# The recurrence of an RWKV-7 layer: receptance products in quarters behind the first pair's features, least distances in the written order, reciprocals in pieces of 64 columns

## The reference, cut to what matters

```python
kk = kk / jnp.maximum(jnp.sqrt(jnp.sum(kk * kk, axis=-1, keepdims=True)), 1e-12)
k_dir = k[None] * (1.0 + (a - 1.0) * k_a)
def step(s, inp):
    r_t, w_t, kk_t, a_t, k_t, v_t = inp
    s_kk = jnp.einsum('bhvk,bhk->bhv', s, kk_t)
    s = (s * w_t[:, :, None, :] - s_kk[..., None] * (kk_t * a_t)[:, :, None, :]
         + v_t[..., None] * k_t[:, :, None, :])
    return s, jnp.einsum('bhvk,bhk->bhv', s, r_t)
# output of a head: (y - mean) / sqrt(var + eps), scaled, plus (r . k_dir) v, times a gate
```

## Time and profile before

| | us |
|---|---|
| median of three runs | 3086.72 (3081.71 to 3093.74) |
| profiled execution | 3085.09 |
| its span | 3083.5 |

### The profile page before, as it was taken

How to read it: one execution, slowest core, us unless ns; L and a number is a source line. 1 busy time by engine, 2 the same in 40 slices (tenths; PEclk the granted TensorE clock), 3 DMA queues, 4 the chain that set the end, 5 groups by cost and what they waited for, 6 DMA issues and landing times. The chain is left out here.

```text
span 3083.5 us, 62817 instructions
## 1 busy us (share of the span) xinstructions
PE 2859.8 (93%) x26751; PEld 2331.1 (76%) x26751; DVE 1897.7 (62%) x3016; ACT 1428.7 (46%) x2197; POOL 526.2 (17%) x482
## 2 busy tenths in 40 slices
PE   7899899998899889999889999999989977999999
PEld 2795677777778658887549999999956744678877
DVE  4941565555665257765778888888864256466652
ACT  1212555655554242221347777777734345343231
POOL 1001545545542010000010000000010045100000
PEclk9999999999999999999999999999989988999999
DMA  5553000000000277655249999999922210222222
GB/s 206 193 191 127 23 21 21 21 21 21 3 3 4 82 255 277 267 198 199 87 153 424 367 369 363 369 367 372 366 99 105 87 36 19 89 77 96 96 96 82
DMA packets 73843, 482.11 MB, mean 156 GB/s; under 512 B 11107, under 2 KB 13027, under 8 KB 32144
## 3 DMA queue, kind: packets, MB, share of 16 engines
q1 hardware_dynamic: 59360, 418.48, 36.0%
q0 software_dynamic: 11952, 51.91, 4.6%
q10 hardware_dynamic: 2304, 8.39, 0.7%
HBM read 457.20 MB, written 34.13 MB: 159 GB/s over the span
## 5 line engine op out<-in xcount | busy, mean ns | idle before, releaser
L2360 DVE TENSOR_TENSOR sb_moe_w_lo<-w_ring,sb_moe_w_hi 128x1408 fp32r<-128x1408 f32 (+1 forms) x132 | 255.3, 1934 | 69.9 <-ACT sb_moe_w_hi L2305 68.3
L2208 PE MATMUL ps<-sb_moe_w_hi,sb_x_feat_lo 128*128 128x352 f32 x832 | 273.4, 329 | 5.2 <-DVE sb_moe_w_lo L2360 5.1
L2210 PE MATMUL ps<-sb_moe_w_hi,sb_x_feat_hi 128*128 128x352 f32 x832 | 267.5, 321 | 0.0
L2209 PE MATMUL ps<-sb_moe_w_lo,sb_x_feat_hi 128*128 128x352 f32 x832 | 266.8, 321 | 0.0
L2305 ACT ACTIVATE sb_moe_w_hi<-w_ring 128x2816 fp32r<-128x2816 f32 x80 | 204.3, 2554 | 2.5 <-DMA w_ring<-w_moe_up 1.8
L2208 PE MATMUL ps<-sb_moe_w_hi,sb_hid_feat_lo 128*128 128x256 f32 x572 | 163.2, 285 | 3.9 <-DVE sb_hid_feat_lo L2491 3.9
L2208 PEld LDWEIGHTS ps<-sb_moe_w_hi,sb_x_feat_lo 128*128 128x128 f32 x832 | 156.1, 188 | 11.5 <-issue 10.4
L2210 PE MATMUL ps<-sb_moe_w_hi,sb_hid_feat_hi 128*128 128x256 f32 x572 | 161.8, 283 | 0.0
L2209 PE MATMUL ps<-sb_moe_w_lo,sb_hid_feat_hi 128*128 128x256 f32 x572 | 161.8, 283 | 0.0
L2209 PEld LDWEIGHTS ps<-sb_moe_w_lo,sb_x_feat_hi 128*128 128x128 f32 x832 | 157.0, 189 | 0.0
L2210 PEld LDWEIGHTS ps<-sb_moe_w_hi,sb_x_feat_hi 128*128 128x128 f32 x832 | 156.0, 187 | 0.0
(11 more groups left out here) (540 smaller groups left out, 7751.2 us busy)
## 6 DMA issues: line engine op xcount, KB each, us to landing
w_ring<-w_moe_up SPq DMA_DIRECT2D x67, 1408.0 KB, 8.4
sb_hm<-w_ada SPq DMA_DIRECT2D x48, 1024.0 KB, 7.1
w_ring<-w_ffn SPq DMA_DIRECT2D x22, 1024.0 KB, 4.9
w_ring<-w_up SPq DMA_DIRECT2D x22, 1024.0 KB, 4.8
sb_b_again<-w_moe_up SPq DMA_DIRECT2D x13, 1408.0 KB, 8.6
sb_hm<-w_moe_up SPq DMA_DIRECT2D x13, 1408.0 KB, 8.2
sb_t_again<-w_moe_up SPq DMA_DIRECT2D x13, 1408.0 KB, 7.7
w_ring<-w_moe_down SPq DMA_DIRECT2D x13, 1408.0 KB, 7.3
```

The source lines that it names most:

```text
L2208: pe.matmul(out, x_lo, w_hi, start=first, stop=False)
L2209: pe.matmul(out, x_hi, w_lo, start=False, stop=False)
L2210: return pe.matmul(out, x_hi, w_hi, start=False, stop=end)
L2360: return V.tensor_tensor(WL[:, s, w], raw[raw_at(c, i)[0]][:, w], WH[:, s, w].bitcast(F32), ALU.subtract)
```

## The change

- The receptance tiles are cut in quarters (two of eight products each), divmod(j, 4) giving tile and part. Two quarters stand ahead of pair 0's Pw0, one ahead of each of Pw1, Pa0, Pa1 and Pnorm, nine ahead of Pg, six ahead of Gkds. The other eleven, with pair 0's Pv and Av0 to Av3 behind the third of them, stand ahead of every second rec entry of the first quad; until they are used up, no feature of pair 1 is placed.
- The tiles come in the order FIRST = (0, 1, 4, 5, 6, 7, 2, 3), and the last three share PSUM bank 5. Loads of r wait for the tile's place in that order. The first score waits for five tiles, the score of the second quad for all eight. The ten keep-warm products are gone.
- behind gives least distances, in rec entries: Pmean 8 behind Gy, Pvar 4 behind Asq, Dbonus 3 behind Pcoef, Pw0 5 behind Dbonus.
- Reciprocals are cut in pieces of 64 columns: twelve for a feature, eight for an output, where six and four were.
- Av is four entries, Av0 to Av3 (waits on v become waits on v3, waits on the output's rec3 waits on rec7), and Pv with them moves from ahead of GB to the end of main.

```diff
@@ -941,8 +941,10 @@
...
 SC_CUTS = ((0, 256), (256, 512), (512, 768))
-REC_CUTS = tuple((a, a + P) for a in range(0, TOK, P))
-OUT_CUTS = tuple((a, a + P) for a in range(0, SEQ, P))
+REC_CUTS = tuple((a, a + CH) for a in range(0, TOK, CH))
+OUT_CUTS = tuple((a, a + CH) for a in range(0, SEQ, CH))
+
+FIRST = (0, 1, 4, 5, 6, 7, 2, 3)
 
@@ -954,10 +956,10 @@
...
         "Asq", "Dscan1.0", "Pnorm", "Dscan1.1", "Aroot", "Dscan1.2", "Gex1", "Drec0", "Gin1", "Drec1", "Drec2",
-        "Drec3", "Drec4", "Drec5", "Dkkn", "APx0", "APi0", "APx1", "APi1", "AP0", "Gkka", "AP1", "APe", "GA", "Pg",
-        "Ag", "Pv", "Av", "GB", "Akd0", "Akd1", "Ark", "Gkdk", "GK", "GR", "Gkds", "Gcoefin"]
+        "Drec3", "Drec4", "Drec5", "Drec6", "Drec7", "Drec8", "Drec9", "Drec10", "Drec11", "Dkkn", "APx0", "APi0", "APx1", "APi1", "AP0", "Gkka", "AP1", "APe", "GA", "Pg",
+        "Ag", "GB", "Akd0", "Akd1", "Ark", "Gkdk", "GK", "GR", "Gkds", "Gcoefin", "Pv", "Av0", "Av1", "Av2", "Av3"]
 late = ["Pcoef", "Dbonus"]
-outs = ["Gy", "Pmean", "Dyc", "Asq", "Pvar", "Aroot", "Drec0", "Drec1", "Drec2", "Drec3", "Gyn", "Aaff", "Gbonus",
+outs = ["Gy", "Pmean", "Dyc", "Asq", "Pvar", "Aroot", "Drec0", "Drec1", "Drec2", "Drec3", "Drec4", "Drec5", "Drec6", "Drec7", "Gyn", "Aaff", "Gbonus",
         "Gated"]
@@ -995,13 +997,17 @@
...
 
+behind = {"Pmean": ("Gy", 8), "Pvar": ("Asq", 4), "Dbonus": ("Pcoef", 3), "Pw0": ("Dbonus", 5)}
 plan, turn = [], 0
 for x in main:
-    if x in ("Pw0", "Pw1", "Pa0", "Pa1", "Pnorm", "Pg"):
-        for n in range(turn, turn + 1 + (x in ("Pnorm", "Pg"))):
-            plan.append(("receptance", 0, n))
-        turn = n + 1
-    plan.append(("feature", 0, x))
+    n = {"Pw0": 2, "Pw1": 1, "Pa0": 1, "Pa1": 1, "Pnorm": 1, "Pg": 9, "Gkds": 6}.get(x, 0)
+    plan += [("receptance", 0, divmod(j, 4)) for j in range(turn, turn + n)]
+    turn += n
+    if x[1:2] != "v":
+        plan.append(("feature", 0, x))
+values = [("feature", 0, x) for x in main if x[1:2] == "v"]
+spare = [("receptance", 0, divmod(j, 4)) for j in range(turn, 4 * 6)] + values + [
+    ("receptance", 0, divmod(j, 4)) for j in range(4 * 6, 4 * N)]
 for p in range(N):
@@ -1019,17 +1025,24 @@
...
         quiet |= {i for i in range(start, ends[q]) if rec[i][1].rstrip("0123456789.") in FRONT[:3]} | set(range(ends[q] - 6, ends[q]))
-    first, turn, stop = 4, ends[0], len(rec) - 16
-    done = [0, 0]
+    first, turn, stop = 8, ends[0], len(rec) - 16
+    done, at_step = [0, 0], {}
     for i, x in enumerate(rec):
+        if p == 0 and i % 2 == 0 and spare:
+            plan.append(spare.pop(0))
+        if spare:
+            plan.append(("rec", *x))
+            continue
         for at, (side, lo, hi) in enumerate(((early, first, turn - 8), (after, turn, stop))):
...
                 continue
-            while done[at] < len(side) and (done[at] < due and (side[done[at]][2][0] != "G" or i not in quiet)
+            while done[at] < len(side) and i - at_step.get(behind.get(side[done[at]][2], ("", 0))[0], -P) >= behind.get(
+                    side[done[at]][2], ("", 0))[1] and (done[at] < due and (side[done[at]][2][0] != "G" or i not in quiet)
                                             or done[at] and side[done[at]][2] in ("Aw0", "Aw1", "Aa0", "Aa1")
...
                 plan.append(side[done[at]])
+                at_step[side[done[at]][2]] = i
                 done[at] += 1
@@ -1113,7 +1126,8 @@
...
             def r_load(p):
-                sp.wait_ge(s_rst[p % 4], 16 * (p // 4 + 1))
+                j = FIRST.index(p)
+                sp.wait_ge(s_rst[j % 4], 16 * (j // 4 + 1))
                 sp.dma_start(r2[:, p % 2, :], A["r_rows"][p]).then_inc(s_r2[p % 2], 16)
@@ -1210,7 +1224,7 @@
...
                 if x == "yn":
-                    pool.wait_ge(o_dve.sem, o_dve.at("rec3", p))
+                    pool.wait_ge(o_dve.sem, o_dve.at("rec7", p))
                     return G.tensor_tensor(YS[:, 0, :], YS[:, 0, :], YS[:, 1, :], ALU.mult)
@@ -1295,7 +1309,7 @@
...
                     pe.wait_ge(o_act.sem, o_act.at("root", p - 2))
-                act("v")
+                act("v3")
                 pe.wait_ge(f_pool.sem, f_pool.at("coefin", p))
@@ -1314,15 +1328,18 @@
...
                 if kind == "receptance":
-                    w = ring.all[:, 2 * KT * P * (x // 2):2 * KT * P * (x // 2 + 1)]
-                    if x % 2 == 0:
-                        pe.wait_ge(s_wr[x // 2], 16)
-                    if x >= 6:
-                        pe.wait_ge(s_re, x - 5)
-                    for k in range(KT):
-                        last = pe.matmul(ps[:, x % 6, :], w[:, (2 * k + x % 2) * P:(2 * k + x % 2 + 1) * P], xr[:, k, :],
+                    j, part = x
+                    m = FIRST[j]
+                    w = ring.all[:, 2 * KT * P * (m // 2):2 * KT * P * (m // 2 + 1)]
+                    if part == 0:
+                        pe.wait_ge(s_wr[m // 2], 16)
+                        if j > 5:
+                            pe.wait_ge(s_re, j)
+                    for k in range(2 * part, 2 * part + 2):
+                        last = pe.matmul(ps[:, min(j, 5), :], w[:, (2 * k + m % 2) * P:(2 * k + m % 2 + 1) * P], xr[:, k, :],
                                          start=(k == 0), stop=(k == KT - 1))
-                    last.then_inc(s_r, 1)
+                    if part == 3:
+                        last.then_inc(s_r, 1)
                     continue
@@ -1348,11 +1365,10 @@
...
                     if n == 0:
-                        pe.wait_ge(s_re, KT)
-                        if p == 0:
-                            self.keep_warm(pe, 3, 10)
+                        pe.wait_ge(s_re, 5 if p == 0 else KT)
                         pe.wait_ge(f_pool.sem, f_pool.at("K", p))
                     if n == CCH:
+                        pe.wait_ge(s_re, KT)
                         pe.wait_ge(f_pool.sem, f_pool.at("R", p))
@@ -1406,7 +1422,7 @@
...
                     else:
-                        pe.wait_ge(f_act.sem, f_act.at("v", p))
+                        pe.wait_ge(f_act.sem, f_act.at("v3", p))
                     for d in range(2):
@@ -1494,17 +1510,15 @@
...
                     return S.activation(PE2[:, u, 1, :], cs[:, 1, :].rearrange("p (c t) -> p c t", t=CH)[:, :, 0], ACT.Copy)
-                if x == "v":
+                if x[0] == "v":
+                    parity, side = divmod(int(x[1]), 2)
                     pe("v")
...
                         act.wait_ge(pe_c.sem, pe_c.at(f"Y{NCH - 1}", p - 2))
-                    for parity, tokens in enumerate(heads):
-                        for side, hh in enumerate(heads):
-                            last = S.activation(
-                                VT[hh, u, :, :].rearrange("p (g c q) n -> p g c q n", g=2, c=3, q=2)[:, :, :, parity, :],
-                                ps[tokens, 6:8, 0:3 * P].rearrange("p g (c h n) -> p g c h n", c=3, h=2)[:, :, :, side, :],
-                                ACT.Copy)
-                    return last
+                    return S.activation(
+                        VT[heads[side], u, :, :].rearrange("p (g c q) n -> p g c q n", g=2, c=3, q=2)[:, :, :, parity, :],
+                        ps[heads[parity], 6:8, 0:3 * P].rearrange("p g (c h n) -> p g c h n", c=3, h=2)[:, :, :, side, :],
+                        ACT.Copy)
                 d = int(x[-1])
@@ -1526,12 +1540,15 @@
...
                 if kind == "receptance":
-                    act.wait_ge(s_r, x + 1)
-                    if x >= 4:
-                        act.wait_ge(s_rst[x % 4], 16)
-                    S.activation(RB[:, x % 4, :], ps[:, x % 6, :], ACT.Copy).then_inc(s_re, 1)
-                    act.wait_ge(s_re, x + 1)
-                    act.dma_start(A["r_rows"][x], RB[:, x % 4, :]).then_inc(s_rst[x % 4], 16)
+                    j, part = x
+                    if part < 3:
+                        continue
+                    act.wait_ge(s_r, j + 1)
+                    if j >= 4:
+                        act.wait_ge(s_rst[j % 4], 16)
+                    S.activation(RB[:, j % 4, :], ps[:, min(j, 5), :], ACT.Copy).then_inc(s_re, 1)
+                    act.wait_ge(s_re, j + 1)
+                    act.dma_start(A["r_rows"][FIRST[j]], RB[:, j % 4, :]).then_inc(s_rst[j % 4], 16)
                     continue
@@ -1588,11 +1605,11 @@
...
                 if x.startswith("rec"):
-                    lo, hi = REC_CUTS[int(x[3])]
+                    lo, hi = REC_CUTS[int(x[3:])]
                     dve.wait_ge(f_act.sem, f_act.at("root", p))
...
                 if x == "kkn":
-                    dve.wait_ge(f_dve.sem, f_dve.at("rec5", p))
+                    dve.wait_ge(f_dve.sem, f_dve.at("rec11", p))
                     return V.scalar_tensor_tensor(out=kk[:, :], in0=kk[:, :], scalar=1e12, in1=kq[:, :], op0=ALU.min, op1=ALU.mult)
```

(4 more changed lines are left out.)

## The result

The changed kernel takes 3092.16 us, median of 19 runs (3086.97 to 3096.79), against 3086.72 for the kernel before (median of 19, 3081.71 to 3094.25). The ratio is 1.0017, 95% interval 1.0010 to 1.0023: 5.4 us slower by the medians, where I had forecast 22.5 us gained. It lies within half a per cent of the kernel before, but above the upper end of my range (3084). The profiled execution's span is 3090.9, 7.4 above before's.

A forecast was written before the change was run, and what follows sets the result against it. TensorE was taken to bound the recurrence stage. Front 5.7, six pairs 15 and pairs 0 and 7 2, less 0.2 at the last output, gave 22.5 us gained: 3062.6 us (3064 against the median), range 3046 to 3084.

The forecast's parts named there:

- First score: Serial front ahead of the pairs: first score starts at 299.3 us, 24.3 earlier, with TensorE deciding.
- Second quad: End of pair 0's first quad: second quad starts at 346.3 instead of 352, gain 5.7 us, bounds 0 and 11.
- Pmean 1.1, Pcoef and Dbonus 1.0: Steady pairs: larger distances and later Pcoef cut TensorE's waits behind Gy, Gcoefin and Dbonus, by 1.1 and 1.0 us a pair.
- Reciprocals 0.5: Steady pairs: halved reciprocals block VectorE half as long, so W waits shrink; 0.5 us a pair, bounds -1 and 1.2.
- V copy 0.9: Steady pairs: V copy in four pieces of 0.49 us shortens X's waits behind ScalarE; 0.9 us a pair.
- The wait of an X behind ScalarE mostly goes: Steady pairs: splitting the V copy mostly removes TensorE's X waits behind ScalarE, 1.1 us a pair.
- Pcoef later: Steady pairs: Pcoef moves later, easing its wait behind Gcoefin; part of the 1.0 us a pair taken with Pw0 behind Dbonus.
- Exponentials 1.0, bounds 0 and 2.5: Third quad's scores: exponentials moved there delay Us of chunk 4 and TensorE's Y4; loss 1.0 us a pair.
- Pairs 0 and 7, 2 us: Pair 0 behind its first quad and pair 7 have part of the waits, together gaining 2 us.
- Period: Time from one steady pair to the next: falls below 87.0 us, to 84.5.
- my 3.5: Steady pairs: the gains 1.1, 1.0, 0.9 and 0.5 us a pair, before the exponentials' loss of 1.0.
- The rival of ScalarE's pile: Third quad's scores: 6.3 us of exponentials on ScalarE make K late and each pair's score wait; 3109 us, chance 0.08.

The follow-up runs named there:

- front_and_v: Changed kernel with whole reciprocals, no distances or empty entries, early part starting at 4 again; new front and V copy at list's end kept: pair 86.95 us, ratio 0.9972.
- whole_spread: The mid_root kernel with whole reciprocals of 128 columns, each followed by an empty entry: pair 85.10 us, ratio 0.9952.
- us_first: The mid_root kernel with one exponential moved behind the copy Us of chunk 4: pair 83.90 us, total 3064.13 us, ratio 0.9923.
- y4_warm: Changed kernel with two unread keep-warm products on TensorE ahead of chunk 4's Y product in pairs 1 to 6: pair 87.40 us, ratio 0.9990.
- root_early: Changed kernel with the features' root moved directly behind Pnorm, ahead of W11's copies: pair 85.34 us, ratio 0.9960.
- order_only: The us_first kernel with whole reciprocals, each followed by an empty entry, and without the least distances: pair 84.54 us, ratio 0.9959.
- before_blanks: Kernel before the change with six empty entries ahead of kkn in a pair's list, so exponentials and kka stand later: pair 89.3 to 90.9 us, ratio 1.0050.
- exp_mid: Changed kernel with the first five of ScalarE's seven exponentials set between reciprocals Drec7 to Drec11: pair 86.81 us, ratio 0.9983.
- mid_root: Changed kernel with both the exp_mid and root_early moves: pair 84.77 us, ratio 0.9926.

## Why the prediction was wrong, step by step

- **First score**: forecast 299.3, measured 299.1. Pw0 idle 4.77 (forecast 4.8), low clock behind it (0.72 from 255 to 260, where it was 1.00 before), the root's end at 273.1 less 1.45 (forecast 272.0), K ready at 298.1 less 1.45 (forecast 297): right, and it was TensorE that decided, as said.
- **Second quad**: forecast 346.3, measured 347.7: gain 4.3 instead of 5.7. The first quad took 48.6 where I had summed 47. Right within its bounds.
- **Pmean 1.1, Pcoef and Dbonus 1.0**: the waits went, 1.24 and 1.3 (1.58 to 0.26). The size was right, the reason mostly wrong: Pmean's wait went by Gy's earlier place, Pcoef's is gone in front_and_v already, which has no distances, and only 0.33 was the distances.
- **Reciprocals 0.5**: right in sum (0.33), with 0.038 us each on VectorE where I took 0.065. But behind it stood the larger effect that I hadn't seen: the same work spread over more entries. W's wait for VectorE (1.06 a pair) is gone whole, in whole_spread too; together with Pmean's, that made the second quad 1.98 shorter.
- **V copy 0.9**: at most 0.4, and 0.08 by itself (front_and_v). The waits of X behind ScalarE in the third quad were 1.14 and Us's 0.48 in before's timeline; those that took their place are 0.57, 0.33 and 0.36. The quad's total hid it.
- **"The wait of an X behind ScalarE mostly goes"** failed. It grew from 10.1 to 18.0 us. I counted what leaves ScalarE's queue and not what arrives: with the early part starting at 8, the root moved past W11, 2.05 us a pair. No term of my sum had it, though the order was there to be read: the prediction's "Pcoef later" comes from the same line.
- **Exponentials 1.0, bounds 0 and 2.5**: mis-sized. The runs give 0.57 (the first ones) + 0.87 (the one ahead of Us) + 1.53 of low clock = 2.97, beyond my bound. The 1.53 goes with the exponentials' wait but also went, in five of six pairs, when only the root was moved. I priced a fall of the clock in the front, behind 4.8 us of idle time, and not here behind 2.5.
- **Pairs 0 and 7, 2 us**: pair 7 gained 3.3, pair 0 behind its first quad lost 1.5: 1.8.
- **Period**: forecast 84.5, measured 88.93. The ledger: 83.90 (us_first) + 0.87 + 0.57 + 2.05 + 1.53 = 88.92. It is a chain of differences between runs, so that it closes shows only that the 1.53 of y4_warm and the third quad's 1.54 of root_early are the same. Without the two misplaced groups the gain is 3.1 of my 3.5. That nearness is in good part luck: order_only, with neither halving nor distances, has 2.5 of it.
- **The rival of ScalarE's pile** had the right engine and place and the wrong victim: kdk still starts behind a gap of 2.54 and K is early. TensorE's own wait for Us decided, and no point had to be passed for that.

Of the 28 us between forecast and result, 27 lie in the six steady pairs. In the stage: 4.3 (front) - 1.5 (pair 0) - 12.2 (six pairs; the first of them was 86.30 before, so 2.6 + 5 x 1.9) + 3.3 (pair 7) = -6.1, which with the 1.45 ahead of the stage is about the span's 7.4.

One row answers the rule that I had weighed against the halving. Reciprocals of the last output, eight of 64 columns, against 3.39 us for four of 128:
```profile
1028.35 3.43 DVE L1626 RECIPROCAL sb_ysum<-sb_ysum 128x64 f32<-128x64 f32 x8 [3.55 <-ACT sb_ysum L1537]
```
Four more instructions cost 0.04 us. The Trainium skill ("VectorE: DVE Perf Modes", the section on the TRN2 errata) has some 0.16 us of fixed latency for each; by that, an estimate from the page, it would have been 0.6. Back to back, the trace doesn't show it.

## What to carry to other kernels

An entry added to a list that is spread over other work moves every entry around it, and so does a later start of the spreading: list, for each engine that works in order, which copy stands behind each moved step before and after, and price the copy's waiter, also for the steps that the change doesn't name. A wait of the bounding engine has two prices, the wait and the clock behind it, and the second can be 1.53 us behind a wait of 2.50, as here, or as much behind a wait of 1.28 (before_blanks). When a change of mixed parts comes out near zero, undo single moves: two reordered groups were worth 5.0 us a pair, more than all parts of the change together.

## What the runs showed of the hardware

- The same wait of 2.50 us of TensorE was followed by about 3.4 us at the lower clock in one pair and by none in the next (root_early), with the work around it the same. In exp_mid and mid_root no fall followed Y4's 1.55, but in before_blanks one followed its 1.28 in two pairs of six. So which waits cost a fall couldn't be foretold from their length; why is open.
- ScalarE loads the table of a root before the root's input is there (load at 515.87, root at 517.85), so in an idle stretch only the 0.81 of the root counts.
- A reciprocal's time goes with its columns down to 64: 0.43 us each in a row, against 0.85 for 128.
- The first quad gained 2.05 where the wait removed was 1.50; the other 0.5 is in TensorE's busy time (30.58 against 30.08 with 684 instructions each at clock 1.00), and why is open.
